# A hybrid decoder layer on one core: ScalarE's SSM steps one key copy later, and the delta rule's masks ahead of two scalings of HGRN2

## The chip, the cores and the metric

The kernel runs on one core of a Trainium2 chip. Its engines work from separate queues and wait for each other on semaphores: TensorE (PE, matmuls into the banks of PSUM), VectorE (DVE), ScalarE (ACT), GpSimd (POOL) and SyncE (SP, which only issues transfers). The metric is the device time of one execution in microseconds.

## What is computed

One layer of a hybrid decoder for a prompt of 512 tokens and 8 samples of 4 tokens, all in float32: a mixer with four parts side by side (MoBA block-sparse attention, Mamba-2 SSM, HGRN2, gated delta rule), then cross-attention to a memory, then a SwiGLU. Cut to what the change touches, the reference is:

```python
# MoBA for the samples: scores against paged keys, best 3 blocks of 256
gate = einsum('bqhd,bnhd->bhqn', q, kmean);  _, idx = top_k(gate, n_sel)
p = softmax(scores of the chosen blocks and of the own tokens);  o = p @ v
# SSM, chunks of 128 tokens
acum = cumsum(ac);  dec = exp(where(mask, acum[l] - acum[s], -inf))
y = einsum(cc, bc, dec, xc) + einsum(cc, h, exp(acum))
h = exp(acum[-1]) * h + einsum(bc, exp(acum[-1] - acum), xc)
# HGRN2: a decay per token and channel
dec = exp(where(mask, bcum[l] - bcum[s], -inf));  att = einsum(qc, kc, dec)
# gated delta rule: a decay per token and head
gam = cumsum(gc);  dec_incl = exp(where(incl, gam[l] - gam[s], -inf))
```

## The kernel before

The program runs in stages (inputs, win, ssm, hgrn, gdn, wout, cross, wxo, wdn), each written out once for every engine. The change lies in the stage called "ssm", which holds the SSM, the sample part of MoBA, HGRN2 and the norms of the delta rule's queries and keys. There are four lanes: "m" (first the SSM, then HGRN2), "p" (the pages of MoBA), "u" (unit norms) and "n" (the SSM's norm). Each lane is a generator on each engine, and `lanes` (lines 3471 to 3476) walks the string `LANES` and runs the next step of the lane that a letter names. All engines walk the same string, so the work of a step stands at the same place of each engine's queue. The order is fixed at build time. The string opens with "pp", then 14 times "mpppp", three times "mppp", one "mpppp", and so on.

In the lane "p", step 1 is small. Step j+2 has on TensorE score j-2 (8 matmuls against the turned keys) and turn j (4 transposes of 128 keys into bank 5 or 6, helper line 267), j from 0 to 63, and on ScalarE copy j of that bank to SBUF (line 1748, recorded under the helper's line 1345). Copy j waits for turn j and for score j-2; turn j waits for copy j-2, score j for copy j. After every 16 scores ScalarE also copies bank 7, a quarter of all scores (j = 17, 33, 49, 65), and the next score waits for that. VectorE does three passes over such a quarter (lines 1705 to 1710). 64 key and value pages come over SyncE's and GpSimd's queues; a key page is asked for when the turns of the page 8 before it are done.

In the lane "m" the SSM (lines 1979, 2078, 2197) goes over 5 tiles: four of 128 prompt tokens, one of the 32 sample tokens. ScalarE's steps are: 1, a table load and the first gate of HGRN2 (line 2213, 2296); 2, 4, 7, 10, 13, `decays`, a copy of a bank (line 2204); 3, 5, 8, 11, 14, `exponentials` of a tile (lines 2210, 2211), with the gate's logarithm behind them in step 3 (line 2299) and its last exponential in step 8 (line 2302); 6, 9, 12 and 15 are empty. VectorE forms the products of a tile when the exponentials are there (line 2092 and tensor_tensor at the helper's line 704); in its step 6 it runs the gate's two operations and two scans (lines 2310, 704, 2314) and then the output of tile 0 (line 2133). TensorE's step 7 (`pre(2)`) has 4 matmuls into bank 0, then spreads the decays of tile 2 into the bank from which VectorE read the output of tile 0: it waits for `ssm_y_out`.

HGRN2 goes over levels j = 0 to 7. On VectorE step j is: differences of level j+2 (`hgrn_diff`), placing of level j (line 2363), `scaled(j+2)` (two products that wait for ScalarE's exponential of that level, line 2195, and let TensorE begin the level), and, for j = 4 and 5, `decay_vector(v, j - 4)`: four operations (line 2669) that subtract and mask the delta rule's decays of tile j-4. ScalarE takes their exponential (line 2674) one step later.

Of the kernel before, what the change touches and what calls it, by code (L numbers as in the profile page):

```python
# [67 lines left out]
def build(nc, a, o):  # L68
# [7 lines left out]
    def S(name):  # L76
        if name not in sems:
            sems[name] = ctx.enter_context(nc.semaphore(name))
        return sems[name]

    with ctx:
# [2115 lines left out]
        def ssm_scalar(s):  # L2197
            def decays(i):
                w = TILES[i][1]
                M = hl(s_m[i % 2], w)  # L2200
                s.wait_ge(S("ssm_pre"), i + 1)
                if i >= 2:
                    s.wait_ge(S("ssm_tile_out"), i - 1)
                A.activation(s_g[i % 2][0:w, 0:2 * w], bank(0)[0:w, 0:2 * w], ACT.Copy)

            def exponentials(i):
                w = TILES[i][1]
                M = hl(s_m[i % 2], w)
                s.wait_ge(S("ssm_m"), i + 1)
                A.activation(s_er[i % 2].rearrange("p a b -> p (a b)")[:, 0:H * w], bank(1 + i % 2)[:, 0:H * w], ACT.Exp)  # L2210
                A.activation(M, M, ACT.Exp).then_inc(S("ssm_exp"), 1)

            s.preload_act_table_set("natural_log_exp_and_others")
            gate_scalar(s, 0)
            yield
            decays(0)
            yield
            exponentials(0)
            gate_scalar(s, 1)
            yield  # L2220
            for i in range(NT):
                if i + 1 < NT:
                    decays(i + 1)
                    yield
                    exponentials(i + 1)
                    if i == 1:
                        gate_scalar(s, 2)
                    yield
                else:
                    yield  # L2230
                    s.wait_ge(S("ssm_samples_mm"), 2)
                    A.activation(s_dec, bank(2)[:, 0:16].rearrange("p (c b) -> p c b", b=NB), ACT.Exp).then_inc(S("ssm_dec_exp"), 1)
                    yield
                    yield
                yield
            yield
            s.wait_ge(S("fin_made"), 1)
            s.dma_start(o["ssm_p"][0, 0].rearrange("(c e) q n -> (e q) c n", e=2), s_fin).then_inc(S("ssm_states_out"), 16)
            s.wait_ge(S("states_made"), 1)
            s.dma_start(o["ssm_s"][0].rearrange("b (c e) q n -> (e q) b c n", e=2), s_h0).then_inc(S("ssm_states_out"), 16)  # L2240
            hgrn_exps(s, 1)
            yield
# [96 lines left out]
        def hgrn_vector(v):  # L2339
            def scaled(j):  # L2340
                v.wait_ge(S("h_dec"), j)
                if j >= 3:
                    v.wait_ge(S("h_lv_mm"), H_MM[j - 2])
                q1, k1 = h_q1[:, (j - 1) % 2], h_k1[:, (j - 1) % 2]
                if j < 3:
                    tt(q1, hq, h_d, ALU.mult)
                    tt(k1, hk, h_d, ALU.mult).then_inc(S("h_qk"), 1)
                else:
                    _, left, right = halves_of(j)
                    tt(right(q1), right(hq), right(h_d), ALU.mult)  # L2350
                    tt(left(k1), left(hk), left(h_d), ALU.mult).then_inc(S("h_qk"), 1)

            def place(j, placed):
                for n_, (i, w) in enumerate(H_JOBS[j]):
                    nm = 4 if w == P else 2
                    level = bc(lev[0:w, min(j, H_PACKED), 0:w].rearrange("p (o l) -> p o l", o=1), (w, nm, w))
                    v.wait_ge(S("h_lv_mm"), H_MM[j] - len(H_JOBS[j]) + n_ + 1 if w == P else H_MM[j])
                    src = h_level_bank(n_, w).rearrange("p (h l) -> p h l", l=w)
                    if j == 0:
                        tt(h_store(i, w), src, level, ALU.mult).then_inc(S("h_lv_out"), 1)  # L2360
                    else:
                        v.wait_ge(S("h_lv_out"), placed)
                        V.copy_predicated(h_store(i, w), level.bitcast(I32), src).then_inc(S("h_lv_out"), 1)  # L2363
                return placed + len(H_JOBS[j])

            placed = 0
            link(tt(lev[:, 6, :], lev[:, 6, :], lev[:, 7, :], ALU.add))
            tt(lev[:, H_PACKED, :], lev[:, H_PACKED, :], lev[:, 6, :], ALU.add)
            scaled(1)
            for j in range(8):  # L2370
                if j + 2 < 8:
                    hgrn_diff(v, j + 2)
                if j == 7:
                    v.wait_ge(S("tail_ebd"), 1)
                    tt(h_kd, hk, h_d, ALU.mult).then_inc(S("tail_prep"), 1)
                if j < H_PACKED or j == 7:
                    placed = place(j, placed)
                if j + 2 < 8:
                    scaled(j + 2)
                if j in (4, 5):  # L2380
                    decay_vector(v, j - 4)
                if j == 6:
                    v.wait_ge(S("h_lv_mm"), H_MM[6])
                    tail_decay_vector(v, 0, h_b, hq, h_q1[:, 1], h_d)
                if j == 0:
                    yield
                yield
            v.wait_ge(S("h_lv_out"), placed)
            tt(lev[:, H_PACKED, :], lev[:, H_PACKED, :], lev[:, 6, :], ALU.subtract)
            tt(lev[:, 6, :], lev[:, 6, :], lev[:, 7, :], ALU.subtract)  # L2390
            yield from hgrn_vector_tail(v)
# [272 lines left out]
        def decay_vector(v, i):  # L2664
            ex, w = g_decay(i), TILES[i][1]
            msk = (negmask if w == P else negmask_s)[0:w, 0:w]
            v.wait_ge(*((S("g_spread"), 64) if i < 2 else (S("g_spread_late"), 48)))
            for h in range(H):
                last = V.scalar_tensor_tensor(ex[:, h, :], ex[:, h, :], cumtok[0:w, i, 4 + h:5 + h], msk, ALU.subtract, ALU.add)
            last.then_inc(S("g_m"), 1)  # L2670
# [781 lines left out]
        def stage(eng, name, *work, enter=True):  # L3452

            n = STAGES.index(name)
            if n and enter:
                eng.wait_ge(S("stage_ended"), 3 * n)
            for f in work:
                f()
            eng.drain().then_inc(S("stage_ended"), 1)

        def mixer_lane(eng, ssm, hgrn):

            yield from ssm
            eng.drain().then_inc(S("stage_ended"), 1)
            yield from hgrn
# [2 lines left out]
        LANES = "m".join(["pp"] + ["pppp"] * 14 + ["ppp"] * 3 + ["pppp", "p", "", "", "ppppppppp"]  # L3468
                         + ["u"] + ["ppppu"] * 4 + ["ppppuun"] * 2 + ["pppp", "p", "p", "np", "", "", ""])

        def lanes(main, pages_, unit, norm):
            steps = {"m": main, "p": pages_, "u": unit, "n": norm}
            for lane in LANES:
                next(steps[lane])
            for lane in "mpun":
                assert next(steps[lane], None) is None
# [38 lines left out]
        @block.scalar  # L3515
        def _(s):
            stage(s, "inputs", lambda: params_loads_scalar(s), lambda: token_squares_scalar(s))
            stage(s, "win", lambda: roots_scalar(s), lambda: small_hi(s),
                  lambda: [win_parts_scalar(s, k) for k in range(4)], lambda: split_hi(s, 1), lambda: params_scalar(s),
                  lambda: [win_parts_scalar(s, k) for k in range(4, KD)], lambda: split_hi(s, NH), lambda: win_scalar(s), enter=False)  # L3520
            stage(s, "ssm", lambda: lanes(mixer_lane(s, ssm_scalar(s), hgrn_scalar(s)), moba_sample_scalar(s), unit_scalar(s), ssm_norm_scalar(s)))
            stage(s, "gdn", lambda: gdn_scalar(s), lambda: gdn_lanes(iter(range(11)), mem_scalar(s)), enter=False)
            stage(s, "wout",
                  lambda: wout_start_scalar(s),
                  lambda: y_gemm_scalar(s, "wout"),
                  lambda: wxq_scalar(s))
            stage(s, "cross", lambda: cross_lanes(cross_prompt_scalar(s), cross_sample_scalar(s)),
                  lambda: cross_out_scalar(s), enter=False)
            stage(s, "wxo",
                  lambda: s.wait_ge(S("mem_kv_out"), 64),  # L3530
                  lambda: y_gemm_scalar(s, "wxo"),
                  lambda: ff_scalar(s), enter=False)
            stage(s, "wdn", lambda: wdn_scalar(s))
# [96 lines left out]
```

## Time and profile before

| | us |
|---|---|
| median of 3 runs | 1222.05 |
| lowest, highest | 1219.35, 1226.39 |
| profiled execution, its own time | 1219.89 |
| its span in the trace | 1218.2 |
| mean granted clock of TensorE | 0.976 of full speed |

| engine | busy us | share of the span |
|---|---|---|
| TensorE matmul | 1159.7 | 95% |
| TensorE weight load | 1010.1 | 83% |
| VectorE | 595.1 | 49% |
| ScalarE | 449.2 | 37% |
| GpSimd | 442.2 | 36% |

Times in the trace are counted from the start of the span. The stage with the change lies between 250 and 425 us. Busy time of TensorE includes matmuls whose ends are modelled, so short waits show best as the idle time in front of an instruction, which the timeline prints in square brackets with the engine that ended it.

### The profile page before, as it was taken

To read this page: it belongs to the slowest core of one execution; us is meant where nothing else is said; L and a number is where in the kernel's file an instruction comes from. 1 tells how busy PE (TensorE), PEld (TensorE's weight loads), DVE (VectorE), ACT (ScalarE), POOL (GpSimd) and SP (SyncE) were. 2 spreads that over 40 slices of the span, in tenths; PEclk is the share of its full clock that TensorE was granted. 3 is DMA by queue.
4 is the path that set the end of the run, shared out by engine and by line. 5 is a ranking of instruction groups with operands and counts; after the bars stand their busy time and mean duration, and the time that the engine had idled before them with its cause. 6 is when DMAs were issued, how large, how long until landed. Compare 5 with 4: busy or idle time off the path is not lost.

```text
span 1218.2 us, 24817 instructions
## 1 busy us (share of the span) xinstructions
PE 1159.7 (95%) x10272; PEld 1010.1 (83%) x10272; DVE 595.1 (49%) x1056; ACT 449.2 (37%) x802; POOL 442.2 (36%) x370
## 2 busy tenths in 40 slices
PE   7999999988998888999989999989999999999998
PEld 6999997865655578888989657989999999977775
DVE  5699744336479887433291552284343433321003
ACT  6323334245534544234552442462222222221212
POOL 8343433153316110453606000614343434333331
PEclk9999999989979998899999999999999999999999
DMA  5332523066659432247414961503332233232222
GB/s 159 98 87 70 177 62 112 27 192 190 187 146 324 149 108 71 88 125 228 123 34 139 289 205 44 153 3 105 87 87 87 87 87 87 70 105 86 77 80 73
DMA packets 176581, 143.45 MB, mean 118 GB/s; under 512 B 15955, under 2 KB 162820, under 8 KB 176214
## 3 DMA queue, kind: packets, MB, share of 16 engines
q1 hardware_dynamic: 166838, 120.44, 33.3%
q0 software_dynamic: 7200, 20.23, 5.3%
q8 instruction: 81, 1.33, 0.5%
q10 hardware_dynamic: 2432, 1.21, 0.3%
q14 instruction: 30, 0.25, 0.1%
HBM read 131.64 MB, written 10.20 MB: 116 GB/s over the span
## 4 chain that ended last, share of the span: by engine, by line
PE 74%; DVE 13%; issue 4%; ACT 4%; POOL 2%; DMA 1%; SPq 1%; POOLq 0%; DVEq 0%; ACTq 0%
PE PS L264 67%; PE PS L267 7%; DVE SC L704 2%; POOL W_LO L248 2%; DVE PROJ L1942 1%; DVE XN L934 1%; DVE XT L704 1%; DVE PROJ L2363 1%; SPq L534 1%; DVE XN L704 1%; DVE XN_parts L924 1%; ACT PROJ L1345 1%; DVE PROJ L1943 1%; DVE PROJ L704 1%; ACT W_HI L239 0%
## 5 line engine op out<-in xcount | busy, mean ns | idle before, releaser
L248 POOL TENSOR_TENSOR W_LO<-W,W_HI 128x1024 fp32r<-128x1024 f32 x128 | 315.1, 2467 | 617.5 <-ACT W_HI L239 617.4
L264 PE MATMUL PS<-XN_parts,W_HI 128*128 128x272 f32 x1184 | 340.6, 288 | 0.0
L264 PE MATMUL PS<-OM_parts,W_HI 128*128 128x272 f32 x960 | 276.3, 288 | 0.0
L264 PEld LDWEIGHTS PS<-XN_parts,W_HI 128*128 128x128 f32 x1184 | 223.2, 188 | 0.0
L239 ACT ACTIVATE W_HI<-W 128x1024 fp32r<-128x1024 f32 x128 | 134.1, 1053 | 206.6 <-PE PS L264 206.6
L264 PE MATMUL PS<-OM_parts,W_LO 128*128 128x272 f32 x704 | 203.9, 290 | 0.0
L264 PEld LDWEIGHTS PS<-OM_parts,W_HI 128*128 128x128 f32 x960 | 180.7, 188 | 0.2
L264 PE MATMUL PS<-SC_parts,W_HI 128*128 128x272 f32 x608 | 179.0, 294 | 1.9 <-POOL W_LO L248 1.6
L264 PE MATMUL PS<-SC_parts,W_LO 128*128 128x272 f32 x608 | 175.9, 289 | 0.0
L264 PEld LDWEIGHTS PS<-OM_parts,W_LO 128*128 128x128 f32 x704 | 132.3, 188 | 0.0
L264 PEld LDWEIGHTS PS<-SC_parts,W_HI 128*128 128x128 f32 x608 | 114.5, 188 | 5.8 <-issue 3.7
L264 PEld LDWEIGHTS PS<-SC_parts,W_LO 128*128 128x128 f32 x608 | 114.4, 188 | 0.0
L264 PE MATMUL PS<-W_HI,PROJ_parts 128*128 128x512 f32 (+1 forms) x320 | 110.6, 374 | 0.0
L264 PE MATMUL PS<-W_HI,SC_parts 128*128 128x256 f32 (+1 forms) x288 | 87.3, 338 | 0.0
L264 PEld LDWEIGHTS PS<-W_HI,PROJ_parts 128*128 128x128 f32 x320 | 61.0, 191 | 13.3 <-issue 2.6
L264 PEld LDWEIGHTS PS<-W_HI,SC_parts 128*128 128x128 f32 x288 | 53.2, 197 | 8.4 <-issue 4.1
L264 PE MATMUL PS<-OM_parts,PROJ_parts 128*128 128x272 f32 x256 | 55.1, 306 | 4.5 <-DVE XN_parts L924 2.4
L704 DVE TENSOR_TENSOR SC<-PS,RSQ 128x544 f32<-128x544 f32 x22 | 15.9, 724 | 88.6 <-PE PS L264 86.7
L264 PE MATMUL PS<-W_LO,SC_parts 128*128 128x512 f32 (+1 forms) x160 | 58.4, 365 | 0.0
L3424 ACT ACTIVATE SC<-SC 128x544 f32<-128x544 f32 x22 | 14.5, 659 | 116.4 <-DVE SC L704 116.4
L704 DVE TENSOR_TENSOR SC<-SC 128x544 f32<-128x544 f32 (+7 forms) x56 | 34.6, 622 | 46.1 <-ACT SC L864 37.3
L1345 ACT ACTIVATE PROJ<-PS 128x512 f32<-128x512 f32 x68 | 40.0, 598 | 37.6 <-PE PS L267 37.6
(406 smaller groups left out, 2067.0 us busy)
## 6 DMA issues: line engine op xcount, KB each, us to landing
W<-in_w_gu SPq DMA_DIRECT2D x44, 512.0 KB, 3.9
W<-in_w_in SPq DMA_DIRECT2D x30, 512.0 KB, 3.8
W<-in_w_down SPq DMA_DIRECT2D x22, 512.0 KB, 3.7
W<-in_w_xkv SPq DMA_DIRECT2D x16, 512.0 KB, 4.1
W_scratch<-in_cache_moba_v SPq DMA_DIRECT2D x36, 128.0 KB, 4.8
W_scratch<-in_cache_moba_v POOLq DMA_DIRECT2D x36, 128.0 KB, 4.9
XT<-in_cache_moba_k SPq DMA_DIRECT2D x32, 128.0 KB, 2.6
XT<-in_cache_moba_k POOLq DMA_DIRECT2D x32, 128.0 KB, 2.5
```

Of the source, the lines that this page charges most:

```text
L239: nc.scalar.activation(hi_lo(n)[0], raw_chunk(n), ACT.Copy)\
L248: nc.gpsimd.tensor_tensor(hi_lo(n)[1], raw_chunk(n), hi_lo(n)[0].bitcast(F32), ALU.subtract).then_inc(S("weights_split"), 1)
L264: return nc.tensor.matmul(out, lhsT, rhs, start=start, stop=stop, skip_group_check=True)
L267: return nc.tensor.transpose(out, in_, ident[0:k, 0:k])
L534: sp.dma_start(dst, src).then_inc(S(name), 16)
L704: return V.tensor_tensor(out, x, y, op)
L924: V.scalar_tensor_tensor(lo(k)[:, TOKENS[run][j]], XT[:, k, TOKENS[run][j]], par(GAINS[run][1] + k), hi(k)[:, TOKENS[run][j]].bitcast(F32) ...
L934: last = V.scalar_tensor_tensor(xn[:, k, c_], xn[:, k, c_], par(GAINS[run][0] + k), rsq[:, c_], ALU.mult, ALU.mult)
L1345: return A.activation(o_, i_, ACT.Copy)
L1942: V.scalar_tensor_tensor(dst[:, d:SEQ], src[:, 0:SEQ - d], wt[3 - d], dst[:, d:SEQ], ALU.mult, ALU.add)
L1943: last = V.scalar_tensor_tensor(ds_, win_[:, :, 3 - d:7 - d], wt[3 - d], ds_, ALU.mult, ALU.add)
L3424: A.activation(f_g[:, t % 2, :], f_g[:, t % 2, :], ACT.Silu).then_inc(S("ff_silu"), 1)
```

## The change

Two edits. The first gives ScalarE its own order of the lanes: in the first 15 places where the string has "mpppp" it has "pmppp". So ScalarE's SSM steps 1 to 14 (and the empty 18) come behind one more step of the lane "p": step k stood behind copy 4k-4 and now stands behind copy 4k-3 (with the score copy where that step has one). TensorE and VectorE keep the string as it was. The second edit swaps two calls in VectorE's HGRN2 steps 4 and 5: the four mask operations come ahead of the two scalings of level 6 and of level 7. No instruction is added or taken away.

```diff
                 if j < H_PACKED or j == 7:
                     placed = place(j, placed)
+                if j in (4, 5):
+                    decay_vector(v, j - 4)
                 if j + 2 < 8:
                     scaled(j + 2)
-                if j in (4, 5):
-                    decay_vector(v, j - 4)
...
+        SCALAR_LANES = LANES.replace("mpppp", "pmppp", 15)
+
-        def lanes(main, pages_, unit, norm):
+        def lanes(main, pages_, unit, norm, order=LANES):
             steps = {"m": main, "p": pages_, "u": unit, "n": norm}
-            for lane in LANES:
+            for lane in order:
                 next(steps[lane])
...
-            stage(s, "ssm", lambda: lanes(mixer_lane(s, ssm_scalar(s), hgrn_scalar(s)), moba_sample_scalar(s), unit_scalar(s), ssm_norm_scalar(s)))
+            stage(s, "ssm", lambda: lanes(mixer_lane(s, ssm_scalar(s), hgrn_scalar(s)), moba_sample_scalar(s), unit_scalar(s), ssm_norm_scalar(s), SCALAR_LANES))
```

## Rows read from the trace of the kernel before

**Rows 1.** The page: the chain that ended last, share of the span by engine.

```profile
PE 74%; DVE 13%; issue 4%; ACT 4%; POOL 2%; DMA 1%; SPq 1%; POOLq 0%; DVEq 0%; ACTq 0%
```

**Rows 2.** Waits of TensorE, 249 to 345 us: waiter, whom for, us, times, longest.

```profile
PE PS L264 <- ACT PROJ L1345: 4.4, 5, 1.4
PE PS L264 <- ACT W_scratch L1345: 4.3, 3, 1.8
PE PS L264 <- DVEq L3459: 0.9, 1, 0.9
PE PS L264 <- DVE W L1691: 0.4, 1, 0.4
```

**Rows 3.** Timeline of ScalarE: start, us, instruction, [idle before]; SSM step 1.

```profile
254.75 1.28 ACT L2213 ACT_TABLE_LOAD   x1
...
256.04 1.11 ACT L2296 ACTIVATE W<-W 128x1088 f32<-128x1088 f32 x1
...
257.06 1.07 ACT L1345 ACTIVATE PROJ<-PS 128x512 f32<-128x512 f32 x2
```

**Rows 4.** Timeline of TensorE: starts behind ScalarE's SSM steps 1, 1, 3, 5, 8.

```profile
257.69 0.65 PE L264 MATMUL PS<-PROJ,W 128*32 128x128 f32 x8 [1.21 <-ACT PROJ L1345]
...
259.32 0.66 PE L264 MATMUL PS<-PROJ,W 128*32 128x128 f32 x8
...
270.50 0.42 PE L264 MATMUL PS<-PROJ,W 128*32 128x128 f32 x8 [1.39 <-ACT PROJ L1345]
...
281.10 0.43 PE L264 MATMUL PS<-PROJ,W 128*32 128x128 f32 x8 [1.82 <-ACT W_scratch L1345]
...
299.49 0.42 PE L264 MATMUL PS<-PROJ,W 128*32 128x128 f32 x8 [1.29 <-ACT PROJ L1345]
```

**Rows 5.** Timeline of ScalarE: fast rhythm, SSM step 5, slow rhythm.

```profile
272.49 0.60 ACT L1345 ACTIVATE PROJ<-PS 128x512 f32<-128x512 f32 x1 [0.35 <-PE PS L267]
...
278.38 0.60 ACT L1345 ACTIVATE PROJ<-PS 128x512 f32<-128x512 f32 x1 [0.35 <-PE PS L267]
...
279.87 0.60 ACT L1345 ACTIVATE PROJ<-PS 128x512 f32<-128x512 f32 x1
...
280.35 0.61 ACT L1345 ACTIVATE W_scratch<-PS 128x512 f32<-128x512 f32 x1
...
283.78 0.60 ACT L1345 ACTIVATE PROJ<-PS 128x512 f32<-128x512 f32 x1 [1.03 <-PE PS L267]
```

**Rows 6.** Timeline of VectorE: products of tile 1, gate, output of tile 0.

```profile
280.01 0.17 DVE L2092 COPY SC<-SC 128x4 f32<-128x4 f32 x1 [3.26 <-ACT SC L2211]
...
284.37 1.29 DVE L2310 SCALAR_TENSOR_TENSOR W<-PROJ,W 128x1088 f32<-128x1088 f32 x1
...
289.53 0.61 DVE L2133 SCALAR_TENSOR_TENSOR OM<-PROJ,SM,PS 128x128 f32<-128x128 f32 x2
```

**Rows 7.** Timeline of TensorE: SSM step 7.

```profile
290.26 0.61 PE L264 MATMUL PS<-PROJ 128*128 128x128 f32 x4
...
290.80 1.15 PE L264 MATMUL PS<-OM,CN 4*128 4x128 f32 x8
```

**Rows 8.** Busy time by stretch of TensorE: stretch, us, PE busy, granted clock, DMA share, GB/s.

```profile
282.00:285.00 3.00, 3.00 (x26) 0.51 0.39 124
```

**Rows 9.** Timeline of VectorE: masks, scaling of level 7, decays of the tail.

```profile
394.43 1.12 DVE L2669 SCALAR_TENSOR_TENSOR SC<-SC,SM,CN 128x128 f32<-128x128 f32 x4
...
398.51 0.69 DVE L704 TENSOR_TENSOR SC<-PROJ,W 128x512 f32<-128x512 f32 x1 [1.12 <-ACT W L2195]
...
404.68 1.29 DVE L704 TENSOR_TENSOR SC<-PROJ,W 128x1088 f32<-128x1088 f32 x1 [1.61 <-ACT W L2258]
```

**Rows 10.** Timeline of ScalarE: exponential of level 7.

```profile
397.42 1.06 ACT L2195 ACTIVATE W<-W 128x1024 f32<-128x1024 f32 x1 [3.05 <-DVE W L704]
```

**Rows 11.** Timeline of TensorE: level 6 of HGRN2.

```profile
402.47 1.08 PE L264 MATMUL PS<-SC 64*32 64x32 f32 x64
```

**Rows 12.** Transfers issued from 355 to 375 us: KB each, us to landing.

```profile
PROJ<-decay_rows SPq DMA_DIRECT2D x2, 272.0 KB, 7.3
```

## The prediction

> **What bounds the kernel now.** I read the chain that ended last, then who TensorE waits for in the stage "ssm", then the timelines of the four engines there, then the clock. TensorE holds 74% of the chain, VectorE 13%, ScalarE 4% [rows 1]: work on another engine counts only where TensorE stands still for it. Between 249 and 345 us TensorE waits for ScalarE's copies 8 times, 8.7 us in all [rows 2]. These are the key copies: turn n puts 4 transposes into one of two banks, copy n brings them to SBUF, and score n and turn n+2 need copy n done. One step of that rhythm takes 0.60 + 0.35 = 0.95 us at 2.4 GHz, of which ScalarE is free for 0.35; at 1.2 GHz it takes 0.60 + 1.03 = 1.63 us [rows 5]. ScalarE work of over 0.35 us that TensorE's own SSM matmuls don't cover makes TensorE wait. The waits stand behind ScalarE's SSM steps 1 (table load and gate), 3 (exponentials and gate), 5 (exponentials, then the copy of a quarter of the scores), 8 and 11: 1.21, 1.39, 1.82 and 1.29 us [rows 4], and for step 11 at most the 0.5 us that the five waits on key copies have left [rows 2]. The other two score copies hold the 2.5 us that are left of the three [rows 2]; no moved step stands ahead of them.
>
> **Part A: ScalarE's order.** The new string puts each of the first 14 SSM steps, and an empty 18th, behind copy 4k-3 where it stood behind copy 4k-4. Nothing is added or removed; TensorE's and VectorE's orders stay. Five of the moved steps are long enough to matter.
>
> Step 1. Now copy 0 is followed by a table load of 1.28, an exponential of 1.11, and copies 1 and 2, 1.07 us for both from 257.06 [rows 3]; TensorE takes score 1 at 257.69 and score 2 at 259.32 [rows 4]. After it, copy 1 runs at once from about 254.63 to 255.23, the load to 256.5, the gate to 257.65, copy 2 to 258.15. TensorE then has score 1 and turn 3 (1.63 us at the low clock) to do meanwhile, from 256.4 to 258.05, and score 2 starts at 258.2 in place of 259.32: **1.1 us gained.** The table load ends and the next activation starts within 0.01 us [rows 3]. The Trainium skill (ScalarE: Activation LUTs, What ACT_TABLE_LOAD costs) adds a drain of about 1.38 us to each load; the trace shows none on either side of this one, and by the page the load would hold the step 1.38 us longer both before and after, so that the gain would be the same.
>
> Step 3. Now ScalarE runs without a break from copy 8 to the end of copy 10, two exponentials and a gate in between. After it, copy 9 waits for turn 9 (0.35 us), then the same work follows: copy 10 ends 0.35 later than now against TensorE, but only score 10 waits for it. Now score 9 starts at 270.50 [rows 4] and score 10 a step later at 271.44; after it, score 10 at 271.3. The wait moves by a step: **0.1 gained.** Steps 8 and 11 are the same case: 0.13 each.
>
> Step 5. Now copy 16 (278.38), two exponentials, copy 17 (279.87), score copy (280.35 to 280.96) [rows 5]; TensorE resumes at 281.10 [rows 4]. After it, copy 17 starts at 279.33 when turn 17 is done, the score copy ends at 280.43, and the exponentials come behind it, under TensorE's next step: **0.65 gained** here. With step 1 and 3, TensorE stands 1.84 us earlier behind step 5.
>
> **What is late next.** The same exponentials feed VectorE. It starts at 280.01 with the products of tile 1, goes on with the three moba passes, from 284.37 with the gate and its scans, and then the SSM output of tile 0, 289.53 to 290.14, with no gap [rows 6]: 10.13 us. TensorE needs that output before it spreads the decays of tile 2: 4 matmuls from 290.26, the spread from 290.80 [rows 7]. So the slack is only 290.80 - 290.14 = 0.66 us. After the change the exponentials are 1.46 us later in ScalarE's order (0.95 for one rhythm step and 0.51 for the score copy) and the whole is 1.2 earlier by steps 1 and 3: 0.26 later on the clock. The output comes at 290.40 and TensorE goes on at 290.45, not at 290.80: **of 1.84 us only 0.35 are left.** TensorE arrives at 288.9 if its clock is low as now, at 286.9 if it isn't, and waits 1.5 or 3.6 us. Steps 8 and 11 then add 0.26. Part A without the clock: -0.6 us.
>
> **The clock.** It fell to half in the stretch 282 to 285, behind the 1.82 us in which TensorE did nothing [rows 8]; two to three key steps there ran at the rhythm of 1.63 us, 0.68 more each, so 1.5 to 2 us were lost. Behind the waits of 1.39 and 1.29 us the next copies keep the fast rhythm [rows 5]. After the change the wait in step 5 shrinks to 1.15, so this fall may go, but that gain only lengthens the wait for VectorE, and a stall of up to 3.6 us is longer than the one behind which it fell. Then one to two key steps behind it run slow: 0 to 1.5 us, mid 0.5. The Trainium skill (TensorE: Matmul & The Clock Gate, What's actually happening) says the gate runs free of the kernel's start; no single trace here can show that, and it would mean that the fall differs between executions of one kernel. **Part A: -0.1 us, bounds -4.1 (no stall for VectorE and no fall) and +2.8 (a long stall, five slow steps).**
>
> **Part B: VectorE's masks.** Four operations of 0.28 (1.12 us) for tile 0 go ahead of the scaling of level 6 (two operations of 0.69 that overlap), and four for tile 1 ahead of that of level 7 [rows 9]. Level 6: VectorE has no gap there, so this only swaps neighbours. The scaling ends 1.1 us later, at 395.6; TensorE takes level 6 at 402.47 [rows 11], 6.9 us later, so 0. The masks need rows that four DMAs on SyncE's queue bring; the slower pair took 7.3 us to land between 355 and 375 us [rows 12], 18 us or more ahead of 393.3: 0; were they late, everything behind them on VectorE would wait too. The difference for level 7 starts where it does now, behind both. Level 7: VectorE stands 1.12 us waiting for ScalarE's exponential, 397.42 to 398.48 [rows 9, 10]; masks of 1.12 us from 397.4 fill exactly that hole, so the scaling starts at 398.5 as now and VectorE is free at 399.8 rather than 400.8. Its next work may start up to 1.0 us earlier, but behind that VectorE already stands 1.61 us for ScalarE's decay exponential, until 404.68 [rows 9], so nothing of it passes on. **Part B: 0, bounds -0.3 and +0.1.** ScalarE's own order of the delta rule's exponentials is unchanged, and it already finds the masks ready.
>
> **What carries on.** Later transfers wait for TensorE's turns or for the stage's end, on SyncE's and GpSimd's queues alike, and TensorE waits for none of them in this stage [rows 2], so a shift passes on as a shift. **Sum:** -0.6 + 0.5 + 0 = -0.1 us on the profiled execution of 1219.89 us (span 1218.2). That execution lies 2.2 us below the median of the three, 1222.05, whose spread is 7 us; I put the forecast at the median less a little: 1221.8.
>
> **Rivals.**
> 1. *The wait for VectorE doesn't bite*: the steps 1, 3, 5, 8, 11 add up, 1.1 + 0.1 + 0.65 + 0.26 = 2.1 us, and the lost clock fall gives up to 2 more: 1218 to 1220. For it: five real waits shrink. Against it: the gapless 10 us on VectorE with 0.66 us of slack. Chance 0.15.
> 2. *Slower: the stall for VectorE makes the clock fall.* Place: TensorE ahead of the decays of tile 2. It decides from a stall over about 1.8 us, since behind 1.82 the clock fell and behind 1.39 it did not. Price: up to five slow steps, 0.68 each, 3.4 us, less the 0.6 gained: 1224.6 at most, 1223 in the middle. Chance 0.25.
> 3. *The change doesn't do what it says*: the steps move, but TensorE's waits only move by one copy each as in step 3, and step 1's too. Then 0: 1222. Chance 0.08.
> 4. *A change of phase elsewhere*: falls of the clock in later stages come and go with the shift, either way by 2 to 3 us, as the spread of three runs does, and together with a drift between sets of runs past 6 us. Chance 0.12, 0.09 of it past 6 us.
>
> **How the numbers follow.** The forecast, a stall for VectorE that eats nearly all, has 0.4. The forecast and rivals 1 to 3 lie inside 4 us of the median before, and a measurement of this kernel can't tell less than about 0.5%, 6.1 us, from no change. Within 0.5%: 0.91; faster 0.05; slower 0.04, both out of rival 4. The range takes in rivals 1 and 2 and the spread of the runs: 1217 to 1226.
>
> **What would show it.** Right: behind step 1 no wait of TensorE; behind step 5 a wait of about 1.15 us; then a new wait of TensorE for the SSM output on VectorE (line 2133) of 1.5 to 3.6 us just ahead of the spread for tile 2; the level 7 scaling with no gap ahead of it, and its end where it was. Wrong: no such wait, and the last key copy 2 us or more earlier; or a mask operation that waits for its DMA; or TensorE waiting for level 6.

## The result and the profile after

The changed kernel takes 1227.66 us (median of 13 runs, 1219.29 to 1234.86) against 1221.17 us before (13 runs, 1219.19 to 1227.69). The ratio is 1.0052, 95% interval 1.0031 to 1.0073: slower, by about as much as the 0.5% that I had called the edge of what can be told. Beside later sets of runs it was 1.0035 (1.0012 to 1.0058) and 1.0054 (1.0026 to 1.0083), so the loss is clear of the noise and some 4 to 7 us. The forecast was 1221.8 us, range 1217 to 1226.

The waits of TensorE between 249 and 345 us, which answer to [rows 2] (waiter, whom for, us, times, longest), from the one profiled execution:

```profile
PE PS L264 <- ACT W_scratch L1345: 3.8, 3, 1.3
PE PS L264 <- ACT PROJ L1345: 3.3, 4, 1.4
PE PS L264 <- DVE OM L2133: 2.7, 1, 2.7
```

The waits for ScalarE's copies fell from 8.7 to 7.1 us. In their place stands one wait that was not there, 2.7 us for VectorE's output of tile 0. TensorE's timeline around it (start, us, instruction, idle before), step 5's score copy and step 7, answering to [rows 4, 7]:

```profile
288.00 0.43 PE L264 MATMUL PS<-PROJ,W 128*32 128x128 f32 x8 [1.27 <-ACT W_scratch L1345]
...
295.73 0.61 PE L264 MATMUL PS<-PROJ 128*128 128x128 f32 x4
...
299.07 1.15 PE L264 MATMUL PS<-OM,CN 4*128 4x128 f32 x8 [2.73 <-DVE OM L2133]
```

And VectorE's chain, as [rows 6]:

```profile
288.89 0.17 DVE L2092 COPY SC<-SC 128x4 f32<-128x4 f32 x1 [4.69 <-ACT SC L2211]
...
293.25 1.29 DVE L2310 SCALAR_TENSOR_TENSOR W<-PROJ,W 128x1088 f32<-128x1088 f32 x1
...
298.41 0.61 DVE L2133 SCALAR_TENSOR_TENSOR OM<-PROJ,SM,PS 128x128 f32<-128x128 f32 x2
```

From 288.89 to 299.02 these are the same 10.13 us without a gap; TensorE goes on at 299.07. The wait for the score copy is 1.27 and not 1.82.

The profiled execution took 1231.97 us, its span 1230.3. It is not to be set against the 1218.2 of before as a whole: compared matmul by matmul, 3.8 of the 12.1 us arise before 30 us, where TensorE's clock stayed low longer, in work that the change doesn't touch. Between 255 and 275 us it was low again, for 17 us; e1 below, another trace with the same waits, had 7 us of that and was 4.3 us faster there. The mean granted clock is 0.965, before 0.976. Busy time by stretch (stretch, us, PE busy, granted clock, DMA share, GB/s), the start, the stretch behind the stall, and the end of the stage, first of before, then of after:

```profile
0.00:200.00 200.00, 189.10 (x1439) 0.99 0.41 113
290.00:345.00 55.00, 50.88 (x638) 1.00 0.66 193
395.00:440.00 45.00, 38.42 (x720) 0.92 0.57 178
```

```profile
0.00:200.00 200.00, 190.43 (x1420) 0.97 0.39 109
290.00:345.00 55.00, 48.15 (x561) 0.97 0.60 175
395.00:440.00 45.00, 39.82 (x668) 0.89 0.61 181
```

Between 290 and 345 us the clock was at 2.4 GHz throughout before; after, it fell to 1.2 GHz behind the stall, from 301.0 for some 3 us. From 395 on there is more low clock too. Part B did what was foretold. VectorE's masks and the scaling of level 7, answering to [rows 9]:

```profile
406.96 1.12 DVE L2669 SCALAR_TENSOR_TENSOR SC<-SC,SM,CN 128x128 f32<-128x128 f32 x4
408.16 0.69 DVE L704 TENSOR_TENSOR SC<-PROJ,W 128x512 f32<-128x512 f32 x1
...
415.12 1.29 DVE L704 TENSOR_TENSOR SC<-PROJ,W 128x1088 f32<-128x1088 f32 x1 [2.69 <-ACT W L2258]
```

The scaling has no idle time in front of it, where 1.12 us stood, and the time saved has gone into the next wait on this line, 2.69 us for 1.61.

### The profile page after: what moved, and what is told of

It is laid out like the page before. It is cut to its first block, busy times and chain, and to the rows that moved or that the text cites. A ratio compares the mean times of both kernels' runs of the same rounds, so it can differ in the third digit from the quotient of the medians.

```text
span 1230.3 us, 24817 instructions
## 1 busy us (share of the span) xinstructions
PE 1171.8 (95%) x10272; PEld 1019.2 (83%) x10272; DVE 595.2 (48%) x1056; ACT 449.0 (36%) x802; POOL 441.7 (36%) x370
## 4 chain that ended last, share of the span: by engine, by line
PE 75%; DVE 13%; issue 4%; ACT 3%; POOL 2%; DMA 1%; SPq 1%; POOLq 0%; DVEq 0%; ACTq 0%
PE PS L264 67%; PE PS L267 7%; DVE SC L704 2%; POOL W_LO L248 2%; DVE PROJ L1942 1%; DVE XN L934 1%; DVE XT L704 1%; DVE PROJ L2363 1%; SPq L534 1%; DVE XN_parts L924 1%; DVE XN L704 1%; ACT PROJ L1345 1%; DVE PROJ L1943 1%; DVE PROJ L704 1%; ACT W_HI L239 0%
```

## The experiments

All ratios are to the kernel before on the same chip, from 6 to 12 runs each; the labels of e9 and e10 carry the times that were planned for their work, the table those that were measured; "behind 290" is the granted clock from 290 to 345 us in the one execution with a profile.

| | kernel | ratio, 95% interval | wait for line 2133, us | clock behind 290 |
|---|---|---|---|---|
| e1 | part A alone | 1.0021 (0.9998 to 1.0043) | 2.7 | 0.97 |
| e2 | part B alone | 0.9999 (0.9975 to 1.0023) | none | 1.00 |
| e3, e12 | changed, gate late | 0.9972 (0.9950 to 0.9995), 0.9983 (0.9963 to 1.0003) | none | 1.00, 0.97 |
| e4 | changed, step 5 back | 1.0012 (0.9984 to 1.0040) | none | 1.00 |
| e5, e15 | before, VectorE held back | 1.0070 (1.0044 to 1.0095), 1.0101 (1.0057 to 1.0146) | 3.1, 4.6 | 0.94, 0.94 |
| e6 | before, gate late | 0.9994 (0.9973 to 1.0015) | none | 1.00 |
| e7 | only step 1 moved | 1.0023 (0.9990 to 1.0056) | 0.8 | 1.00 |
| e8 | only step 5 moved | 1.0028 (1.0002 to 1.0055) | 2.7 | 0.94 |
| e9 | before, 0.65 us more work | 0.9999 (0.9981 to 1.0018) | none | 1.00 |
| e10 | before, 2.5 us more work | 1.0020 (0.9997 to 1.0043) | none | 1.00 |
| e11, e16 | changed, again | 1.0035, 1.0054 (above) | 2.7, 2.7 | 0.94, 0.97 |
| e13 | changed, wait filled | 1.0038 (1.0005 to 1.0070) | 0.8 | 1.00 |
| e14 | held back, wait filled | 1.0058 (1.0035 to 1.0080) | 0.8 | 0.97 |

The theory after the result (stall theory): step 5's exponentials, one key copy later, hold VectorE back, TensorE stands idle for its output, and the idleness brings the low clock. The rivals: step 1's shift keeps the clock low at the stage's start (start theory); part B does it (mask theory); a mere shift of the stage meets the clock differently (phase, shift or arrival theory).

**Which part.** e1 keeps only the second and third hunk of the diff, e2 only the first.

> ScalarE's order alone, VectorE's masks where they were. Stall theory (TensorE's 2.73 us wait for VectorE's output of tile 0 and the clock behind it) and start theory (step 1's shift leaves TensorE's clock low longer at the start of the stage) both expect the whole loss, about 1.005 of the kernel before, the 2.7 us wait there again, and a fall of the clock within 5 us behind it. Mask theory (part B brings the two extra low stretches at 410 to 418 and 430 to 435 us) expects 1.002 to 1.003 and only one low stretch between the last key copy and the delta rule.

> VectorE's masks alone, ScalarE's order as before. Stall and start theories expect 1.000 (within 0.002) and the scaling of level 7 with no idle time ahead of it. Mask theory expects 1.002 to 1.003 and more than one low stretch of TensorE's clock between 395 and 430 us.

e2 gives 0.9999: the masks cost nothing, though its interval would hide 3 us either way. e1 has the whole mechanism, the 2.7 us wait and the fall behind it; its 1.0021 lies under the 1.005 that I expected, and its interval, 0.9998 to 1.0043, takes in no loss at all as well as much of what the changed kernel lost. That e1 also had much low clock from 395 to 440 us (0.81) with the masks in their old place speaks against the mask theory a second time.

**Take the stall away.** e3 is the changed kernel with VectorE's gate behind the output and state of tile 0; e6 has the same edit in the kernel before:

```diff
-                if i == 0:
-                    gate_vector(v, 1)
                 if w == NS:
...
                 v.drain().then_inc(S("ssm_tile_out"), 1)
+                if i == 0:
+                    gate_vector(v, 1)
                 yield
```

e4 leaves the gate and puts only step 5 back behind copy 16:

```diff
-        SCALAR_LANES = LANES.replace("mpppp", "pmppp", 15)
+        SCALAR_LANES = LANES[:22].replace("mpppp", "pmppp") + LANES[22:27] + LANES[27:].replace("mpppp", "pmppp", 10)
```

> The changed kernel with VectorE's gate and scans behind the output and state of tile 0 instead of ahead of them. Stall theory: no wait of TensorE for line 2133, the stage 2.7 us or more shorter than in the changed kernel, no low clock at 300 us, ratio to the kernel before 0.997 to 0.999. Start theory: the stall was only 2.7 of the loss, the low stretch at the start of the stage stays at 10 us or more, ratio 1.002 to 1.003. Mask theory: ratio about 1.002.

> The changed kernel with VectorE's gate and scans behind the output of tile 0, once more, to see whether its gain over the kernel before holds. Ratio 0.996 to 0.999, no wait for line 2133 and no low clock at 300 us.

> The kernel before with only VectorE's gate and scans behind the output of tile 0. Stall theory: TensorE has 0.66 us of slack there already, so nothing or up to 0.4 us is gained, ratio 0.999 to 1.000, and the changed ScalarE order is what brought the gain of the kernel with both. If the gate's place alone brings the gain: 0.997.

> The changed kernel with ScalarE's SSM step 5 back behind copy 16, all else as changed. Stall theory: VectorE gets its exponentials 1.46 us earlier in ScalarE's order, TensorE's wait for line 2133 falls from 2.73 to under 1 us, TensorE's wait for the score copy goes back to about 1.8 us, ratio about 0.999 to 1.001. Start theory: ratio 1.003 to 1.005, since step 1 is still moved.

In e3 TensorE takes the spread for tile 2 with no wait, and its only waits on other engines' SSM and key work are the seven on ScalarE. The two rows are its step 7 and its stretch behind 290:

```profile
295.65 1.15 PE L264 MATMUL PS<-OM,CN 4*128 4x128 f32 x8
```

```profile
290.00:345.00 55.00, 50.88 (x605) 1.00 0.65 197
```

With the same ScalarE order, the kernel now comes out ahead of the one before: 0.9972 and 0.9983 (the second interval just reaches 1.0003), medians 1218.57 and 1218.47 us, the fastest tried. The same order with the gate early took 1223.68 (e1) and 1224.82 us (e11) beside them on the same chips. Alone, the late gate gives 0.9994; that interval overlaps those of e3 and e12, but the table of stretches further down shows the gain of ScalarE's order on the trace, 2.2 us, once VectorE no longer stands in its way. The start theory expected 1.002 to 1.003 for e3 and falls: e3's profiled execution had the long low stretch at the stage's start (clock 0.76 from 250 to 285 us, as the changed kernel), e2 with the old ScalarE order had it too, and e1 and e12 with the new order had not (0.90 and 0.95). It comes and goes with the execution. e12's 0.97 is a short low stretch at 342 us; at 300 us its clock was full, as expected. e4 removes the wait for line 2133 entirely (expected: under 1 us) and goes to 1.0012, inside the error of either 0.9990 or 1.0030; it alone decides nothing.

**Make the stall alone.** e5 and e15, one kernel, repeat three of five scans, with no order changed:

```diff
-                    for c_ in range(2):
-                        last = V.tensor_tensor_scan(h_b[:, c_, :], keep[:, :], h_d[:, c_, :], 0.0, ALU.mult, ALU.add)
-                    link(last)
+                for again in ((0, 1), (0, 1), (0,)):
+                    for c_ in again:
+                        last = V.tensor_tensor_scan(h_b[:, c_, :], keep[:, :], h_d[:, c_, :], 0.0, ALU.mult, ALU.add)
+                    link(last)
```

(The kernel has two scans; the repeats make five.) e8 moves only step 5 of ScalarE, e7 only step 1.

> The kernel before, with three of the gate's five scans done again on VectorE (three repeats, the same values), which holds the SSM output of tile 0 back by about 3.3 us; no order is changed. Stall theory: TensorE waits 2.5 to 2.9 us for line 2133 and the clock falls within 5 us behind it; ratio 1.002 to 1.004. Phase theory (the loss comes from a shift of the whole stage against the clock, whatever shifts it): ratio within 1.001 of the sum of the wait itself, 1.0023, with extra low stretches behind 400 us in some executions.

> The kernel before with the three repeated scans, TensorE idle for 3.1 us, once more beside the filled one. Both theories: 1.005 to 1.008.

> The kernel before with only ScalarE's SSM step 5 (exponentials of tile 1) one key copy later. Stall theory: TensorE gains 0.55 at the score copy, then waits for line 2133: VectorE's chain ends 1.46 later against 0.66 of slack, so TensorE resumes 0.8 us later than before, plus the fall of the clock; ratio 1.001 to 1.003. Start theory: 1.000.

> The kernel before with only ScalarE's SSM step 1 (table load and gate) one key copy later. Stall theory: 1.1 to 1.3 us gained at 257 us and kept, since VectorE's chain moves with it; no wait for line 2133 above 0.3 us; ratio 0.998 to 0.9995. Start theory (this step keeps the clock low longer at the stage's start): ratio 1.001 to 1.003 and a low stretch over 10 us in front of 275 us.

```profile
298.36 2.07 PE L264 MATMUL PS<-OM,CN 4*128 4x128 f32 x8 [3.08 <-DVE OM L2133]
```

```profile
290.00:345.00 55.00, 47.80 (x544) 0.94 0.56 170
```

This is e5: a wait of 3.08 us, and the clock from 290 to 345 us at 0.94. The row itself took 2.07 us at the low clock, in e3 1.15. The ratio is 1.0070 and in the repeat 1.0101, 8 to 12 us for a wait of 3 to 4.6: more than either theory had said. (In e15's trace the wait is 4.59 because its clock did not fall behind the 1.81 us wait at the score copy, so TensorE came to the spread 1.4 us sooner.) e8 shows that step 5 alone makes both the wait and the loss, 1.0028 where 1.001 to 1.003 was expected. e7 missed. TensorE reached the spread 1.3 us sooner than before, but only 0.7 of that stood ahead of step 5; the fall of the clock near 282 us did not come in its profiled execution, so TensorE came another 1.4 us earlier and waited 0.75 us of it for VectorE: the slack of 0.66 was used up by the clock alone. Its ratio, 1.0023 with a wide interval, is that of two groups: 9 of its 12 runs took 1218 to 1224 us, 3 took 1231 to 1236. Its low stretch in front of 275 us was not over 10 us.

**Delay without idleness.** e9 and e10 repeat transposes of turn 50 in the kernel before; e13 and e14 repeat 18 and 21 transposes of turn 24, just where TensorE would wait, in the changed kernel and in e5's:

```diff
-                for i in range(4):
+                for i in [k % 4 for k in range(10 if j == 50 else 4)]:
```

(27 in place of 10 for e10; 22 and 25, and j == 24, for e13 and e14.) The expectations put a repeated transpose at 0.15 us. It took 0.11: turn 50 of e10, and the same turn before,

```profile
327.78 3.17 PE L267 MATMUL PS<-CN,XT 128*128 128x128 f32 x27
...
328.03 0.66 PE L267 MATMUL PS<-CN,XT 128*128 128x128 f32 x4
```

are 2.5 us apart and not 3.4. So e9 added 0.65 us, e10 2.5, e13 2.0 and e14 2.3, and 0.8 us of wait was left in each of the last two.

> The kernel before with 6 transposes of turn 50 done again (same data, same bank), some 0.9 us more work for TensorE at about 331 us and no wait at all. Stall theory (the loss is the wait for VectorE and the fall right behind it): 0.9 us more, ratio 1.0007. Shift theory (what comes later depends on when the stage arrives, since TensorE's clock falls in some executions at 405 to 436 us and in others not): more than the work itself, 3 to 6 us, ratio 1.002 to 1.005, with low stretches of 6 us or more between 400 and 440 us.

> The same with 23 transposes again, some 3.4 us more work. Stall theory: 3.4 us, ratio 1.0028. Shift theory: what counts is the point of arrival and not the size, so about its own 3.4 us or a little more, and not four times what the small delay costs.

> The changed kernel with 18 transposes of turn 24 done again (same data, same bank), some 2.65 us of work, in the place of TensorE's 2.73 us wait for line 2133. Idleness theory: the wait shrinks to under 0.4 us, no low clock behind it, and the kernel is faster than the changed kernel beside it by 1.5 us or more for all its added work, ratio to the kernel before 1.000 to 1.002. Arrival theory: no difference to the changed kernel, 1.004.

> The kernel before with the three repeated scans on VectorE, and 21 transposes of turn 24 done again, some 3.1 us of work, in the place of TensorE's 3.1 us wait. Idleness theory: ratio 1.002 to 1.003, the 3.1 us themselves. Arrival theory: 1.006 to 1.007 as without the filling.

> The changed kernel once more, beside the others on one chip. Both theories: ratio 1.003 to 1.006, TensorE's wait for line 2133 of 2.7 us. Shift theory: the low stretches behind 400 us differ from those of the first trace of this kernel though all waits are the same.

> The changed kernel beside the filled one. Both theories: 1.003 to 1.005, the wait of 2.7 us for line 2133, low clock behind it.

The delays cost themselves: 2.5 us of work makes 1.0020 (its own share is 1.0021), 0.65 us makes 0.9999. The shift theory falls as a rule, although the single trace of e9 does show the low stretches that it foretold (clock 0.85 from 395 to 440 us); such a stretch in one execution is no mean. So 2.5 us of added work cost 2.4 us (interval -0.4 to 5.3), where a wait of 3.1 us had cost 8.5 (5.4 to 11.6). The place differs, though, 328 us against 295; the filled kernels put the work where the wait was. e14, its repeated transposes of turn 24 and then the spread:

```profile
290.10 2.95 PE L267 MATMUL PS<-CN,W_scratch 128*128 128x128 f32 x25
...
294.33 1.15 PE L264 MATMUL PS<-OM,CN 4*128 4x128 f32 x8 [0.84 <-DVE OM L2133]
```

Filled, the kernel held back took 1227.81 us in the median, unfilled beside it 1234.56 (six runs); the mean granted clock over all their runs is 0.9716 and 0.9648. That pair differs by more than its scatter, but against e5, the same unfilled kernel on another chip, the filled one hardly does: 1.0058 and 1.0070. The changed kernel filled took 1224.01, unfilled 1226.34, clocks 0.9726 and 0.9697, which the scatter of 12 runs each covers. And the ratios, 1.0058 and 1.0038, are close to those that the arrival theory had named (1.006 to 1.007, 1.004); the 1.002 to 1.003 that the idleness theory gave to e14 lies outside its interval, 1.0035 to 1.0080, and its 1.000 to 1.002 for e13 meets only the lower end of its interval, 1.0005 to 1.0070.

The traces say a little more. e13's has the clock of e1 up to the spread and no fall behind it, and TensorE was 1.5 us ahead of e1's at the next score copy for all its added work. e14's had a low stretch at 296 us behind a wait of only 0.84 us, and it cost 1.5 us there, as in e1. So filling the wait took away the fall in one of two traces, and that it is the idleness, and not the late spread, that makes the loss larger than the wait is not shown.

## Why the prediction was wrong

- *Steps 1, 3, 5, 8, 11 on ScalarE.* From copy 0 to copy 3 TensorE gained 1.0 us (e7) to 1.3 (e1) by step 1, for 1.1. The wait there was 0.33 and not none in the changed kernel. But by copy 16, just ahead of step 5, only 0.7 us of it was left in e1 and e7 and 0.5 in e16 (counted from TensorE's 0.87 us wait for L3459), where the sum carried 1.2. All traces have a low stretch over step 1, and in which work it falls changes with the step; that this eats the difference is likely, not shown. Step 5's wait came to 1.27, for 1.15. Steps 3, 8 and 11 gave nothing, where 0.36 in sum was expected: their waits moved by one copy with their full size. So the 1.84 us behind step 5 were 1.1 to 1.2, and of the 0.35 that was to be left at the spread nothing was: it came 0.1 to 0.3 us later than before (e1, e16).
- *VectorE is late next.* Right in kind, place and sequence: a chain of 10.13 us, TensorE waiting for line 2133 in step 7, 2.73 us where I had 1.5 or 3.6. The 3.6 took the fall at 282 us for 2.0; from the score copy to TensorE's arrival before the spread the kernel before took 9.70 us with the fall and e7 8.34 without it, 1.4. e3 and e8 show that step 5 and the gate in front of the output are its two causes.
- *The clock: the step that failed.* I put the stall's consequence at 0 to 1.5 us, mid 0.5. The low clock right behind the stall cost 1.4 to 2.9 us. In all seven traces with a wait of 2.7 us or more for line 2133 (changed three times, e1, e5, e8, e15) the clock was low between 290 and 345 us, 0.97 or 0.94. In the other traces it was 1.00, but for e14 and for the late stretch of e12. The fall at 282 us that the change does away with was worth little, since in the kernel before it lay beside VectorE's chain: TensorE, had it been faster, would have stood there (0.75 of the 1.4 us in e7).
- *The threshold.* I took a stall over about 1.8 us as what makes the clock fall, from 1.82 us with a fall and 1.39 without. The later traces don't bear it out: behind the wait of 1.81 or 1.82 us it fell in 8 of 10 traces, not in e7 and e15, and behind that of 1.39 it did fall in e1, e11 and e13. e1, the wait and the clock behind it:

```profile
269.39 0.42 PE L264 MATMUL PS<-PROJ,W 128*32 128x128 f32 x8 [1.39 <-ACT PROJ L1345]
...
272.00:275.40 3.40, 3.40 (x26) 0.50 0.76 231
```

- *The loss behind that.* A term that the sum did not have. Some of it shows from 395 to 440 us: of the seven, five had over 10 us of low clock in HGRN2's last part and the start of the delta rule, e15 9.4 and e8 5.2, but e6, e7, e9, e10 and e14 of the others had over 10 too, of which e6 and e9 cost nothing in the mean. e11's trace, with the same waits as the first, stands at 0.81 there where that stood at 0.89:

```profile
395.00:440.00 45.00, 40.16 (x620) 0.81 0.51 157
```

- *Rival 2*, slower because the stall makes the clock fall, is the one that came true. Its place and cause were right, its threshold was not. I gave it 0.25 and a middle of 1223, 1224.6 at most; the measured 1227.66 lies 3 us above. I capped it by the first fall alone.
- *Rival 1*, no wait for VectorE, 1218 to 1220: that is e3, whose median is 1218.57.
- *Rivals 3 and 4.* Steps 3, 8 and 11 did only move their waits by a copy, as rival 3 says, but step 1 did not. Rival 4 had low clock in later stages come and go with the shift; what the sum lacks lies there, and whether the shift or chance brings it is open.
- *Part B.* Right on each point, and zero within the error (e2).
- *The range* ended at 1226, 1.7 us too low. It took the spread of the runs before for granted; the changed kernel's own runs spread nearly twice as far, to 1234.86.

**What the stall costs on the traces.** Counted from the start behind TensorE's 0.87 us wait for L3459 (250.54 us before), with the granted clock over the first stretch, in us:

| trace | clock up to the spread | up to the spread | from there to the score behind the next score copy | sum |
|---|---|---|---|---|
| before | 0.87 | 40.26 | 14.52 | 54.78 |
| e2, masks alone | 0.77 | 44.11 | 14.52 | 58.63 |
| changed | 0.81 | 44.69 | 15.92 | 60.61 |
| e3, changed, gate late | 0.80 | 41.93 | 14.52 | 56.45 |
| e1, part A alone | 0.92 | 40.40 | 15.97 | 56.37 |
| e16, changed | 0.92 | 40.56 | 15.96 | 56.52 |
| e13, changed, filled | 0.92 | 40.39 | 14.52 | 54.91 |

The changed kernel and e3 ran at nearly the same clock up to the spread: the stall costs 2.8 us there and 1.4 behind it, 4.2 in all. Against the old order, paired by the length of the low stretch ahead of step 5 (17 us: changed and e2; 7 us: e1, e16 and before), the changed order stands only 1.6 to 2.0 us later, since its gains went into the wait; e3 stands 2.2 ahead of e2. That is about the gain that e3 and e12 have over many runs (3.4 and 2.1 us by the ratios), but only 1.6 to 2.0 of the 4 to 7 us that the changed kernel loses.

**What stays open.** The rest, 2 to 5 us, arises later. From that score to the end of the execution the seven traces with the stall took 912.6 to 921.7 us, the others 909.7 to 915.4 but for e10 (920.4 without its added work), so the two groups overlap. 13 of 37 runs of the changed kernel lie above 1230 us, none of the 24 of e3 and e12 and none of the 140 of the kernel before; but e4, e7 and e13, with little or no stall, have 3 of 12 each. Why low clock later on is commoner behind the stall is not settled, nor whether idleness or lateness brings it. Nor was it tried to keep TensorE busy through the whole wait.

## What to carry to other kernels

When one engine's order is moved against the others, follow each moved result to every reader, and give the slack of the slowest one first: here 1.46 us of delay met 0.66 us of slack, and moving VectorE's gate, which nobody needed yet, turned a loss of 0.5% into a gain of 0.2 to 0.3%. A wait of the bounding engine should be priced with what its clock does right afterwards, which here cost as much as half of the wait to the whole of it; a filler should be timed before it is relied on (0.11 us for a transpose here, not 0.15); and where single executions of one kernel differ by 10 us, a trace locates a wait but only many runs price it.

## What the runs showed of the hardware

- At a wait of TensorE of 2.7 to 4.6 us for line 2133 the clock fell to 1.2 GHz in 7 of 7 traces, within 2 us behind its end or, in e5, e11 and e15, already during it. Behind a wait of 1.81 or 1.82 us it fell in 8 of 10, behind one of 1.39 us in 3 of 18 (e1, e11, e13), behind those of 1.27 to 1.30 us, from 270 to 345 us, in none.
- A TensorE delay of 2.5 us made of work cost about itself (1.0020; its share is 1.0021), waits of 3.1 to 4.6 us, elsewhere in the stage, 8 to 12 us (1.0070, 1.0101).
- A wait filled for the most part with repeated transposes went with a mean granted clock of 0.9716 and a median of 1227.81 us, unfilled with 0.9648 and 1234.56 beside it (e14, e15), but with 0.9692 and 1230.36 on another chip (e5); in the changed kernel the difference, 2.3 us, is inside the scatter (e13, e16). Repeated transposes took 0.11 us each at 2.4 GHz.
- The clock from 250 to 285 us was 0.76 to 0.95, depending on the execution and not on the order. The Trainium skill (TensorE: Matmul & The Clock Gate, What's actually happening) says that the gate runs free of the kernel's start; two executions of the changed kernel with the same waits, at 0.89 and 0.81 from 395 to 440 us, agree with it.
